# Hybrid gMLP and band-attention step: feature-major projections in pairs by Strassen's scheme

## The reference

```python
h = jnp.einsum('bsd,de->bse', x, w_in)
u_a = gelu(h[..., 0:512]);  v_a = layernorm(gelu(h[..., 512:1024]))
z_a, q, k, v_b, z_b = h[..., 1024:1536], ..., h[..., 3072:3584]
a_out = u_a * (tril(w_s) @ v_a per 128-frame chunk and 128-channel group + b_s)
b_out = banded softmax attention of q, k, v_b, 8 heads of 64, 8 chunks back
y = concatenate([a_out * silu(z_a), b_out * silu(z_b)]) @ w_out
return layernorm(ALPHA * x + y)
```

## Time and profile before

| what | value |
|---|---|
| median of 3 runs | 1058.67 us (1057.13 to 1059.17) |
| span of the profiled execution | 1056.0 us |
| what lies around the span (median less span) | 2.7 us |
| PE busy | 1045.7 us, 99% of the span |
| DVE, ACT, POOL busy | 453.3, 359.5, 130.9 us |
| opening, until chunk 0 is done | 0 to 19.6 us |
| va's tiles | 56 to 161.6 us |
| the 18 single groups | 161.6 to 585.3 us |
| v's first 13 tiles | 585.3 to 656 us |
| attention, output projection, end | 656 to 1056 us |

### The profile page before, as it was taken

The page is one execution under the profiler, slowest core; times in us unless marked ns, Lnnn a source line. Parts: engine busy times, 40 slices in busy tenths (PEclk is TensorE's granted clock), DMA queues, the critical chain, the costliest instruction groups (busy, mean ns, idle before and its releaser), DMA issues.

```text
span 1056.0 us, 17699 instructions
## 1 busy us (share of the span) xinstructions
PE 1045.7 (99%) x7342; PEld 909.4 (86%) x7342; DVE 453.3 (43%) x956; ACT 359.5 (34%) x728; POOL 130.9 (12%) x144
## 2 busy tenths in 40 slices
PE   8999999999999999999999999999999999999997
PEld 7988889999999999999999888777888888888885
DVE  6634442202021211111113000487777777776665
ACT  6511001111111111111112111566666666666630
POOL 0111111120101000000000000004222222223201
PEclk9999999999999999999999999999999999999999
DMA  9661113222221333434342143594444444433222
GB/s 336 204 195 40 40 40 118 90 69 65 91 61 55 97 115 113 122 115 134 115 140 70 45 151 115 183 318 138 144 147 153 134 142 144 148 111 111 91 80 80
DMA packets 105087, 128.43 MB, mean 122 GB/s; under 512 B 7192, under 2 KB 76464, under 8 KB 105008
## 3 DMA queue, kind: packets, MB, share of 16 engines
q1 hardware_dynamic: 100544, 112.62, 32.8%
q10 hardware_dynamic: 4464, 14.68, 4.3%
HBM read 82.17 MB, written 48.26 MB: 124 GB/s over the span
## 4 chain that ended last, share of the span: by engine, by line
PE 99%; DMA 1%; DVE 0%; issue 0%; SPq 0%; DVEq 0%; ACT 0%
PE s_ps L1277 35%; PE out_ps L1489 17%; PE s_ps L1294 16%; PE pt_ps L1277 8%; PE o_ps L1451 6%; PE s_ps L1380 5%; PE pt_ps L1422 3%; PE pt_ps L1294 2%; PE s_ps L1489 2%; PE s_ps L1409 1%; PE o_ps L1306 1%; PE out_ps L1306 1%; DMA x_raw<-x_t 1%; PE o_ps L1465 0%; PE s_ps L1326 0%; PE s_ps L1330 0%
## 5 line engine op out<-in xcount | busy, mean ns | idle before, releaser
L1277 PE MATMUL s_ps<-xh,ring 128*128 128x384 f32 (+1 forms) x1152 | 327.6, 362 | 0.0
L1277 PEld LDWEIGHTS s_ps<-xh,ring 128*128 128x128 f32 x1152 | 212.4, 188 | 22.8
L1277 PE MATMUL s_ps<-xl,ring 128*128 128x384 f32 (+1 forms) x576 | 208.7, 362 | 0.0
L1294 PE MATMUL s_ps<-ring,xh 128*128 128x512 f32 x480 | 149.7, 393 | 0.0
L1277 PEld LDWEIGHTS s_ps<-xl,ring 128*128 128x128 f32 x576 | 108.1, 188 | 11.5
L881 ACT ACTIVATE prob<-prob,low 128x640 f32<-128x640 f32 (+3 forms) x128 | 97.5, 763 | 47.7 <-DVE low L1112 47.7
L1112 DVE CUSTOM_DVE_ANT_1 prob<-s_ps,bias 128x640 f32<-128x640 f32 (+1 forms) x112 | 85.7, 803 | 58.9 <-PE s_ps L1380 58.7
L1294 PEld LDWEIGHTS s_ps<-ring,xh 128*128 128x128 f32 x480 | 88.7, 188 | 18.3 <-issue 0.3
L1489 PE MATMUL out_ps<-wo_h,yh 128*128 128x512 f32 x248 | 100.5, 405 | 0.0
L1489 PE MATMUL out_ps<-wo_h,yl 128*128 128x512 f32 x248 | 97.0, 391 | 0.0
L1489 PE MATMUL out_ps<-wo_l,yh 128*128 128x512 f32 x248 | 96.9, 391 | 0.0
(11 more groups left out here) (155 smaller groups left out, 1339.7 us busy)
## 6 DMA issues: line engine op xcount, KB each, us to landing
raw<-w_all ACTq DMA_DIRECT2D x26, 512.0 KB, 3.6
r<-x SPq DMA_DIRECT2D x17, 512.0 KB, 3.7
q<-s_q SPq DMA_DIRECT2D x16, 512.0 KB, 3.9
k<-s_k SPq DMA_DIRECT2D x16, 512.0 KB, 5.6
y_out<-r SPq DMA_DIRECT2D x15, 512.0 KB, 2.7
x_raw<-x_t SPq DMA_DIRECT2D x12, 384.0 KB, 14.3
s_mix<-st SPq DMA_DIRECT2D x17, 256.0 KB, 2.3
v_all<-st SPq DMA_DIRECT2D x17, 256.0 KB, 2.1
```

The lines of the kernel that those rows point to most:

```text
L1277: last = nc.tensor.matmul(bank[b][:, 0:width], w[:, kc, :], xx[:, kc, :], start=kc == 0 and a == 0, stop=kc == KC - 1 and a == 2)
L1294: last = nc.tensor.matmul(out, xx[:, kc, cols], ring[:, 0:GRP, side, kc, :], start=kc == 0 and a == 0, stop=kc == KC - 1 and a == 2)
```

## The change

1. **Strassen.** Groups are taken in pairs (`PAIRS`, ten of them: 256 features) and tokens in two blocks. The weight of a pair is 2 x 2 blocks (feature group x half of the 1024 inputs), x is 2 x 2 blocks (half of the inputs x token block). Seven block products in Winograd's form replace eight. Each of the seven has an own weight operand (four need sums, made by POOL) and an own x operand (four need sums, made by POOL), and each operand is split into high and low part.
2. **Two passes.** The seven x operands don't fit in SBUF for all tokens. Pass 0 takes two blocks of 512 tokens, pass 1 two blocks of 576 (2 x 288 columns, because a bank holds 512). Each pass runs all ten pairs.
3. **Putting together.** Products 0, 2 and 4 accumulate in one PSUM sum, which ACT copies out after each of them (`copy_sum`); DVE adds a copy to a PSUM sum for each of the four results of a pair (`add_sums`) and puts it in SBUF. gelu, tanh and the second passes (`hand`, `finish_unit`) then read SBUF instead of PSUM.
4. **Token-major tiles** no longer find x in SBUF: each tile loads its 128 tokens again (`x_tiles`, two buffers, two halves of 256 KB), and they are split again.
5. **Order.** va's 17 tiles, pass 0, v's tiles 0 to 7, pass 1, v's tiles 8 to 12, attention with v's last four tiles. The bias of the mixing moves from DVE to ACT (copy, `copy_mix`) and POOL (addition, `add_bias_s`). va's and v's weights share SBUF with the pairs' operands, piece by piece.
6. LayerNorm parameters load at the start; POOL's preparation of the attention bias waits for the end of pass 1.

The core of the diff:

```diff
+PASSES = 2
+WIDTH = [512, 576]
+SPLIT = [1, 2]
+PAIRS = [("u", 0), ("za", 0), ("u", 2), ("za", 2), ("k", 0), ("k", 2), ("q", 0), ("q", 2), ("z", 0), ("z", 2)]
+SUM_OF = [0, 2, 0, 1, 0, 3, 2]
+V_MID = 8
+LAG = 4
+def step_builds(step):
...
+    b, p_b = divmod(step - LAG, OPS)
+    if step - LAG >= first and b + 1 < (pas + 1) * NP:
+        out.append(("op", b + 1, p_b))
+    return out + [("piece", pas + 1, j) for j in PIECES_IN.get(last - step, ())]
+PIECES_IN = {4: (0,), 3: (1,), 2: (2,), 1: (3, 4)}
+PIECES_AFTER = [5, 7, 6]
+X_IN_TILE = [{}, {}]
+for _j in range(21):
+    X_IN_TILE[0].setdefault(5 + _j // 2, []).append((_j // 7, _j % 7))
+X_IN_TILE[0].setdefault(16, []).extend([(3, 0), (3, 1), (3, 2)])
+for _j in range(28):
+    X_IN_TILE[1].setdefault(min(1 + _j // 4, V_MID - 1), []).append((_j // 7, _j % 7))
```

TensorE:

```diff
+            def product(m, p):
+                pas = m // NP
...
+                pe.wait_ge(w_ready, BUILT["op", m, p])
+                if p == 0 and m:
+                    pe.wait_ge(copied, 3 * m)
+                if p == 1 and m:
+                    pe.wait_ge(added, 4 * m)
+                if p in (2, 4):
+                    pe.wait_ge(copied, 3 * m + p // 2)
+                if p == 6:
+                    pe.wait_ge(added, 4 * m + 2)
+                n = WIDTH[pas] // SPLIT[pas]
+                for c in range(SPLIT[pas]):
+                    out = sums[SUM_OF[p]][:, c, 0:n]
+                    for kc in range(HK):
+                        for a, (side, xx) in enumerate(((0, xo_h), (0, xo_l), (1, xo_h))):
+                            made = nc.tensor.matmul(out, wf[:, p, side, kc, :], xx[pas][p][:, kc, c * n:(c + 1) * n],
```

VectorE, in va's tiles, between the passes and in a pass:

```diff
             for t in range(TILES):
...
+                if t + 2 < TILES:
+                    xt_low_part("va", t + 2, 0)
+                if t < TILES - 1:
+                    for kc, p in X_IN_TILE[0].get(t, ()):
+                        xo_low_part(0, kc, p)
                 dve.wait_ge(vn_centred, 2 * t + 2)
                 dve.wait_ge(rstd_v_ready, t + 1)
...
+                if t + 2 < TILES:
+                    xt_low_part("va", t + 2, 1)
...
+                    if p >= 4:
+                        finish_unit(4 * m + p - 4)
+                    if p == 0 and step > first:
+                        finish_unit(4 * m - 1)
+                    for what in step_builds(step):
+                        w_low_part(what)
...
+                    add_sums(m, p)
+                for j in PIECES_AFTER[:2]:
+                    w_low_part(("piece", pas + 1, j))
+                finish_unit(4 * NP * (pas + 1) - 1)
...
+                    for t in range(V_MID):
+                        for kc, p in X_IN_TILE[1].get(t, ()):
+                            xo_low_part(1, kc, p)
...
+                        for h in range(2):
+                            if t + 2 < V_MID:
+                                xt_low_part("v", t + 2, h)
```

GpSimd:

```diff
             for t in range(TILES):
+                if t >= 1:
+                    sum_x(0, t - 1)
+                if t >= 2:
+                    add_bias_s(t - 2)
                 pool.wait_ge(mv_v_ready, t + 1)
...
+                if 12 <= t < 15:
+                    sum_w(0, t - 12)
...
+                        if m + 1 < first + NP and p >= 4:
+                            for i in ((0, 1), (2,), (3,))[p - 4]:
+                                sum_w(m + 1, i)
...
+                if pas == 0:
+                    for j in range(16):
+                        sum_x(1, j)
+                    for i in range(3):
+                        sum_w(NP, i)
```

SyncE at the end of a pass:

```diff
+                store_unit(4 * NP * (pas + 1) - 1)
+                sp.wait_ge(added, 4 * NP * (pas + 1))
+                t = V_MID * pas + 1
+                for h in range(2):
+                    load_xt("v", t, h)
```

More of the change, by code:

```diff
@@ L104, in stores @@
         place[event] = [(s, count[s]) for s in slots]
         for s in slots:
-            count[s] += 1
+            count[s] += each
+    for event in EVENTS:
+        if event[0] == "va":
+            staged(event, [2 + event[1] % 2], 2 if event[1] == TILES - 1 else 1)
+            if event[1] == TILES - 1:
+                staged(("gv",), [0], 1)
+        elif event[0] == "v":
+            if event[1] in (0, V_MID):
+                place["before", event[1]] = list(count)
+            staged(event, [2 + event[1] % 2], 1)
+            turn = 0
+        elif event[2] >= 3:
+            n = 4 * event[1] + event[2] - 3
+            pas, kind = unit_of(n)[:2]
+            if kind != "u":
+                n_slots = 2 if kind in "qk" else 1
+                staged(("unit", n), [(turn + j) % 4 for j in range(n_slots)], 2 if pas and kind in ("z", "za") else 1)
+                turn += n_slots
@@ new lines, with builds @@
+FIRST_EARLY = [0, 1, 2, 4, 5]
+PIECES_IN = {4: (0,), 3: (1,), 2: (2,), 1: (3, 4)}
+PIECES_AFTER = [5, 7, 6]
+def builds():
+    out = [("piece", 0, j) for j in KO]
+    for pas in range(PASSES):
+        out += [("op", pas * NP, p) for p in FIRST_EARLY]
+        for step in range(pas * NP * OPS, (pas + 1) * NP * OPS):
+            out += step_builds(step)
+        out += [("piece", pas + 1, j) for j in PIECES_AFTER]
+    return {what: n + 1 for n, what in enumerate(out)}
+BUILT = builds()
+X_IN_TILE = [{}, {}]
@@ new lines, with xt_buffer, xt_loads_before, xt_user_before @@
+XT_ORDER += [("v", t, h) for t in range(TILES) for h in range(2)]
+XT_COUNT = {half: n + 1 for n, half in enumerate(XT_ORDER)}
+def xt_buffer(kind, t):
+    seq = tile_seq(kind, t)
+    if seq % 2:
+        return 1
+    return 2 if kind == "v" and t > V_MID else 0
+def xt_loads_before(kind, t):
+    seq = tile_seq(kind, t)
+    return sum(tile_seq(*e) % 2 == seq % 2 and tile_seq(*e) < seq for e in EVENTS if e[0] in ("va", "v"))
+def xt_user_before(kind, t):
+    held, seq = xt_buffer(kind, t), tile_seq(kind, t)
+    had = [e for e in EVENTS if e[0] in ("va", "v") and xt_buffer(*e) == held and tile_seq(*e) < seq]
+    return had[-1] if had else None
@@ L1050, in _ @@
+            w_low_part(("piece", 0, KO[0]))
+            for t in range(2):
+                xt_low_part("va", t, 0)
+            for j in KO[1:3]:
+                w_low_part(("piece", 0, j))
+            for t in range(2):
+                xt_low_part("va", t, 1)
+            for j in KO[3:]:
+                w_low_part(("piece", 0, j))
             dve.wait_ge(lnv_loaded, 48)
@@ L1093, in _ @@
+            for t in range(V_MID, V_EARLY):
+                for h in range(2):
+                    xt_low_part("v", t + 2, h)
             dve.wait_ge(far_ready, 3)
@@ L1352, in scores @@
+            for t in range(V_MID, V_EARLY):
+                project_tile("v", t, 0, 2)
             def scores(unit):
@@ L1413, in turn @@
                 if unit == 0:
[L1414 removed]
+                    pe.wait_ge(added, NUNITS)
                 else:
```

1164 lines of the change are left out of this document (697 added, 467 removed).

## The result

| | kernel before | changed kernel |
|---|---|---|
| median of the runs | 1058.6 us (1057.1 to 1059.2, 4 runs) | 1077.5 us (1075.0 to 1080.2, 4 runs) |
| ratio, 95% interval | | 1.0188 (1.0166 to 1.0210) |
| span of the profiled execution | 1056.0 us | 1073.2 us |

A forecast was written before the change was run, and what follows sets the result against it. PE, busy 99% of the span, was taken to bound the kernel. Matmuls 52.7 us less, stalls and other terms 49.5 us more, made 3.2 us less than the old 1058.7: 1055 us, range 1024 to 1084.

The forecast's parts named there:

- va's tiles: Stage before pass 0: POOL's sums and bias put between DVE's steps cost 15 us, between 1 and 21.
- What bounds, and the price of a matmul: Projection stages: PE sets the time; matmuls cost 0.2267 us at 512 columns, 0.1335 at 288, saving 52.7 us.
- Rival D: Pass 1: 288 columns are too few to cover a load, 0.188 us each; 1144 us, chance 0.03.
- The mechanism: DVE and POOL run one after the other; a POOL product between DVE instructions costs DVE 1.0 us.
- The end: End of va's tiles: first product waits behind DVE's last three x splits and first weight split, 1 us.
- Nothing for: Work costed at zero, including the attention's same tiles with four more splits on each of ACT and DVE.
- Between the passes: v's tiles 0 to 7: late loads, and DVE splits alternating with POOL sums, cost 19.5 us, between 6 and 26.
- After pass 1: v's tiles 8 to 12: the same end of a pass plus v11's late load, 6.5 us, between 2 and 9.
- the clock: Lower granted clock after PE's stall before v9: 1 us lost, between 0 and 6.
- pass 0 and pass 1: Stalls inside the passes: 6 us in pass 0 (0 to 14), 2.5 us in pass 1 (0 to 6).
- Rival C: Port shared by DVE and POOL becomes the bound in va, between the passes and pass 0; 1076 us, chance 0.25.

The follow-up runs named there:

- e_wgate: Changed kernel with the 80 weight-block sums and 16 gatings of u moved from POOL to DVE: 1063.2 us, ratio 1.0061 to the kernel before.
- e_last: e_buf with DVE making pass 1's first two weight low parts before the last four token blocks: 1024.1 us, ratio 0.9690 to the kernel before.
- e_extra: e_three and e_wgate combined, plus 16 useless 128x512 sums on POOL from v's first tile on: 1048.8 us, against 1036.3 without those sums.
- e_skew: Changed kernel with s_skew's eight broadcasts moved from va's tile 7 to pairs 1 to 4 of pass 0: 1072.4 us, ratio 1.0147 to the kernel before.
- e_three: Changed kernel with e_xsum's edit, the mixing's bias as one DVE sum, and s_skew's broadcasts in pass 1: 1045.0 us, ratio 0.9884 to the kernel before.
- e_attnp: Changed kernel with the low-part splits of v's tiles 15 and 16 moved from DVE to POOL: 1077.0 us, ratio 1.0186 to the kernel before.
- e_buf: e_three and e_wgate combined with v1's and v9's loads earlier (1037.8 us), plus a third buffer for v's tiles 9 to 16: 1028.4 us.
- e_xsum: Changed kernel with all 32 sums of token blocks moved from POOL to DVE: 1063.2 us, ratio 1.0065 to the kernel before.

## Why the prediction was wrong

The forecast of slightly faster failed by its stalls: 49.5 us forecast, 72.8 measured, in a sum where 3.2 us decided. Of the 23.3 us between, 9.6 lie in va's tiles, 6.2 in the attention, 3.8 between the passes and 3.7 in the other stages.

*What bounds, and the price of a matmul: right.* Pass 1 in e_wgate and e_last, nearly without stalls, takes 222.7 us for 1680 matmuls, 0.1326 each against my 0.1335. Rival D is excluded. Of the 52.7 us saved at least 50.7 are real: in e_last pass 0 takes 194.1 and pass 1 222.7, stalls and two mixings included, against 467.5. As a whole e_last is 32.5 us under the kernel before.

*The mechanism: right.* I read the exclusion off one overlap and put 1.0 us on a POOL sum set between DVE's instructions. e_extra measured 0.87 us. So that price was not too low; what else went wrong is below. The idles came where I had put them: at v0 (0.4 us), v1 (3.7), v3 (5.9), v4 (4.1) and v9 (3.8).

The Trainium skill (SBUF — State Buffer, Who interferes with whom) has two SBUF inputs on DVE and a GpSimd read excluding each other for the whole instruction, and a DVE instruction with at most one SBUF input going free outside its 2-port modes. The trace agrees with the second part: the addition that reads PSUM took 0.68 us wholly under a POOL sum at 236.90, where the split just before it took 1.78. For the first part the measured 0.87, of the 1.28 that POOL's product takes alone, says that DVE isn't held for all of it.

*The step that failed first: va's tiles, 15 us forecast, 24.6 measured.* I listed what the change adds to a tile and left out what stood in SP's list beside it: the eight broadcasts. The kernel before issued them at nearly the same time, 58.87 us, but there x was resident, no tile's load shared the queue, and the first mixing result was stored only at 76.10. That is the 7.84 us idle, and a granted clock of 0.82 over the 28 us from 62 on: 16.7 us between two mixings in place of 6.35, 10.3 us that my sum had at nothing. The term that I did have was too large. I let every tile from 5 to 14 overrun by 1.05 us, 11 us, and added 3 for the weight sums; in fact the tiles ran at 6.35 up to 99.3, one took 6.8, and only the three with a weight sum took 7.92, some 5 us in all. With two POOL operations DVE needs 6.9 us a tile (e_skew, 93.76 to 100.66) and not 7.3. So the miss of 9.6 us is what is left of larger errors of both signs. The end took 4.2 us where I had 1, and the first tile after the opening waited 2.8 us for a split that DVE had behind a tile's statistics (22.63), for which I had nothing.

*What this hid.* The two limits hide each other, as e_three shows: 5.5 us for the broadcasts alone, 0 and 3.1 for two of DVE's reliefs alone, 17.4 for all three.

*The second step: the attention, nothing forecast, 6.2 us measured.* "The same tiles in the attention, four more splits" stood under "Nothing for", as work that fits beside the rest. But x was resident before, and now each of the tiles 13 to 16 must be loaded into a buffer that its predecessor but one has just left. e_attnp showed that moving the splits gains nothing, e_buf that the loads issued earlier give the 6 us back.

*Between the passes: 19.5 forecast, 23.3 measured.* The right mechanism and nearly the right size. From the pass's end I had the operands at 13 us, DVE's alternation with POOL from 20 on, and 45 us for it: 65, of which I entered 63 at the low end. Measured are 14.4 (POOL's first sum at 351.59), 21.1 (DVE's first split of an operand at 358.31) and 66.8. So 2 us are my rounding down, 1 us is the later start, and less than 1 us the alternation, whose pairs took 1.8 us (16 sums in 29.2) where I had 1.7 to 1.75. One thing came out by chance: DVE sets the pace only up to v5 (387.5), the last three tiles are PE's own 16.6 us, and DVE's list ends together with them.

*After pass 1: 7.5 with the clock, 8.8 measured; pass 0 and pass 1: 6 and 2.5, 7.2 and 2.7 measured.* Sizes near, pass 1 by luck: with e_wgate it took 222.7 us, so its matmuls alone are at most that, and it had cost 4.3 us beyond them and not 2.7; my price of a matmul was 1.6 us too high for the pass.

*Rival C* had the mechanism and the total, 1076, but partly for wrong reasons: its 61 us in va, between the passes and in pass 0 were 55.1, its 9 for the rest 17.7. The chance I gave it, 0.25, came from "my sum allows nothing for gaps"; the gaps were not it: in va's slow tiles DVE is busy 7.85 of 7.92 us. Nor was the port alone: 10.3 of va's 24.6 us and the attention's 6.2 came from late loads and stores.

## What to carry to other kernels

Before work goes to GpSimd because it looks idle, look at what VectorE does at the time: if its instructions read two operands from SBUF, each 512-element GpSimd sum that meets them costs it nearly a microsecond, more than doing the sum itself (0.7 us). Where a change makes a resident operand into a streamed one, follow each load to the buffer it waits for, and list what else stands in that queue. And expect limits that hide each other: fixing one of them alone measured 0, 3.1 and 5.5 us where all three gave 17.4.

## What the runs showed of the hardware

- A useless 128x512 sum on POOL cost DVE 0.87 us; in back-to-back alternation each engine got one instruction per 1.63 to 1.65 us, where alone they take 1.28 and 0.76. The pair is 0.4 us shorter than the two in sequence, so hand-overs overlap by an estimated 0.2 us each.
- DVE additions that read one operand from PSUM took no longer under a POOL operation: 32 of 80 ran wholly under one, none of the 80 took more than 0.76 us.
- A single tile as input doesn't make a DVE instruction free: in the attention 87 of the 96 products of `prob` and the scalar `rden` (640 elements) took 0.55 us, and the nine that began under a POOL product of 2.4 us took 2.0 to 2.6.
- 288-column matmuls with a weight load each start 0.1326 us apart, though a load's recorded length is 0.188 us.
- Eight broadcasts of 384 KB, issued in 5.3 us by one queue, delayed the store and the loads issued behind them: 11.1 us from issue to landing, where the median of such loads was 3.0. TensorE stood for 7.8 us. In pass 1 no cost was seen (228.0 us in e_three, 228.3 in e_xsum without them).
